# Inverting the delta-net chunk matrices: first level from a masked transpose, second factor turned by TensorE, level mask on the product

## The reference, cut to what matters

```
a = jnp.where(strict, einsum("bhnid,bhnjd->bhnij", kb, k) * decay, 0.0)
t_inv = triangular_solve(a + eye, eye, left_side=True, lower=True, unit_diagonal=True)
u = t_inv @ (v * beta[..., None])
w = t_inv @ (kb * jnp.exp(g)[..., None])
# then a scan over the chunks with the state s
```

## Time and profile before

| | us |
|---|---|
| median of three runs | 1910.13 (1909.71 to 1915.04) |
| the profiled execution, its own time | 1912.29 |
| its span | 1910.4 |
| PE, DVE, ACT, POOL busy in the span | 1774.9, 938.4, 631.0, 184.4 |
| first start and last end of the level products u, tt, ti | 1413.98, 1491.84 |
| first start of a `TT` product | 1492.48 |

### The profile page before, as it was taken

How to read it: one execution, slowest core, us unless ns; L and a number is a source line. 1 busy time by engine, 2 the same in 40 slices (tenths; PEclk the granted TensorE clock), 3 DMA queues, 4 the chain that set the end, 5 groups by cost and what they waited for, 6 DMA issues and landing times.

```text
span 1910.4 us, 25378 instructions
## 1 busy us (share of the span) xinstructions
PE 1774.9 (93%) x9992; PEld 1329.9 (70%) x9992; DVE 938.4 (49%) x1704; ACT 631.0 (33%) x1183; POOL 184.4 (10%) x202
## 2 busy tenths in 40 slices
PE   5999999899999999899989999899889789989998
PEld 2443445378888886343679998566579679879997
DVE  2134764343434343255636664444579853545544
ACT  3112643232313232134625443213322144034443
POOL 1001000100000001042000001001159100000000
PEclk8999999999999999999989999799899999999999
DMA  9224774322222232334034443223120234334442
GB/s 380 76 90 155 284 286 156 132 89 88 89 89 88 93 121 109 116 133 176 24 151 177 177 179 140 80 108 122 62 105 1 89 133 177 127 138 177 163 152 83
DMA packets 20885, 253.87 MB, mean 133 GB/s; under 512 B 2208, under 2 KB 4512, under 8 KB 5024
## 3 DMA queue, kind: packets, MB, share of 16 engines
q1 hardware_dynamic: 17712, 242.44, 33.4%
q10 hardware_dynamic: 3056, 9.82, 1.4%
HBM read 251.20 MB, written 1.05 MB: 132 GB/s over the span
## 4 chain that ended last, share of the span: by engine, by line
PE 84%; DVE 8%; ACT 3%; issue 2%; DMA 2%; POOL 1%; DVEq 0%; POOLq 0%; ACTq 0%
PE bank L491 26%; PE bank L517 13%; PE bank L519 13%; PE bank L518 13%; PE bank L912 6%; PE bank L575 3%; PE bank L649 3%; PE bank L672 2%; PE bank L657 2%; DVE w_lo L1558 1%; POOL root L2001 1%; ACT w_hi L1157 1%; DMA x<-in_x 1%; PE bank L628 1%; PE bank L636 1%
## 5 line engine op out<-in xcount | busy, mean ns | idle before, releaser
L491 PE MATMUL bank<-slab,weights 128*128 128x256 f32 (+2 forms) x1456 | 450.7, 469 | 8.2 <-ACT slab L1097 6.1
L491 PEld LDWEIGHTS bank<-slab,weights 128*128 128x128 f32 (+1 forms) x1456 | 277.5, 192 | 176.4 <-issue 142.8
L1558 DVE TENSOR_TENSOR w_lo<-weights,w_hi 128x1024 fp32r<-128x1024 f32 (+1 forms) x220 | 264.3, 1211 | 95.9 <-ACT w_hi L1157 95.0
L517 PE MATMUL bank<-h_hi,w_hi 128*128 128x256 f32 (+1 forms) x864 | 278.9, 323 | 25.4 <-DVE h_lo L1579 15.1
L1157 ACT ACTIVATE w_hi<-weights 128x1024 fp32r<-128x1024 f32 (+1 forms) x220 | 228.3, 1046 | 214.6 <-PE bank L519 209.5
L519 PE MATMUL bank<-h_hi,w_lo 128*128 128x256 f32 (+1 forms) x864 | 275.6, 319 | 0.0
L518 PE MATMUL bank<-h_lo,w_hi 128*128 128x256 f32 (+1 forms) x864 | 275.1, 318 | 0.0
L517 PEld LDWEIGHTS bank<-h_hi,w_hi 128*128 128x128 f32 x864 | 165.7, 192 | 41.1 <-issue 29.5
L517 PE MATMUL bank<-mlp_hidden_hi,w_hi 128*128 128x512 f32 (+1 forms) x512 | 174.8, 341 | 0.6 <-DVE w_lo L1558 0.6
L519 PEld LDWEIGHTS bank<-h_hi,w_lo 128*128 128x128 f32 x864 | 165.0, 191 | 12.8
L518 PEld LDWEIGHTS bank<-h_lo,w_hi 128*128 128x128 f32 x864 | 165.8, 192 | 11.6
(11 more groups left out here) (206 smaller groups left out, 2334.7 us busy)
## 6 DMA issues: line engine op xcount, KB each, us to landing
weights<-in_ada SPq DMA_DIRECT2D x36, 2048.0 KB, 7.6
weights<-in_mlp_up SPq DMA_DIRECT2D x16, 2048.0 KB, 8.5
weights<-in_mlp_down SPq DMA_DIRECT2D x16, 2048.0 KB, 8.4
weights<-in_ffn_in SPq DMA_DIRECT2D x11, 2048.0 KB, 7.6
weights<-in_in SPq DMA_DIRECT2D x8, 2048.0 KB, 8.3
weights<-in_gate SPq DMA_DIRECT2D x6, 2048.0 KB, 7.7
weights<-in_ffn_out SPq DMA_DIRECT2D x8, 1408.0 KB, 5.8
weights<-in_even_in SPq DMA_DIRECT2D x4, 2048.0 KB, 11.7
```

What stands on the lines that cost most here:

```text
L491: last = mm(b[rows, 0:width], lhsT(k), rhs(k), start=k == 0, stop=k == kc - 1)
L517: mm(b[:, 0:width], wh, hi(k), start=k == 0, stop=False)
L1558: V.tensor_tensor(split_part(w_lo, q), raw_part(q), split_part(w_hi, q).bitcast(F32), ALU.subtract)\
```

## The change

All in the inverse. (1) POOL's fill of X and Y with the identity is gone. (2) The first level is not run as a step: PE turns `Amat[:, t]` (group `a`), DVE writes `Y = -(turned) * between0` from the bank and adds the identity. (3) `X` is no longer kept: group `tr` turns Y by four transposes, and DVE writes `XR = tr * within` from the bank (`other_root`). (4) `lev` is gone: PE multiplies with the unmasked `Amat`, and the mask comes on the product, in the copy out of the bank, which DVE now does in ACT's place (`ubuf = u * between`). (5) POOL makes YR, in DVE's place. (6) `ti` and its subtraction are gone. 24 steps are left (`STEPS`).

```diff
+        STEPS = 4 * (len(LEVELS) - 1)
...
-            def level_products(n):
...
+            def turned(tag, src):
+                b = open_group(tag)
+                for hd in range(DN_HEADS):
+                    ins = nc.tensor.transpose(b[:, hs(hd)], src[:, hs(hd)], ident)
+                close(ins, tag)
+
+            def level_step(n):
+
+                if n < STEPS:
+                    t = n % 4
+                    pe.wait_ge(sem("YR_ready"), n + 1)
+                    heads(("u", n), lambda hd: Amat[:, t, hs(hd)], lambda hd: YR[:, n % 3, hs(hd)])
+                if 1 <= n <= STEPS:
+                    j = n - 1
+                    t = j % 4
+                    drained(pe, ("tr", j))
+                    drained(pe, ("u", j))
+                    heads(("tt", j), lambda hd: XR[:, t, hs(hd)], lambda hd: ubuf[:, j % 2, hs(hd)])
+                if 2 <= n < STEPS - 2:
+                    j = n - 2
+                    drained(pe, ("tt", j))
+                    turned(("tr", j + 4), Y[:, j % 4, :])
...
+            for t in range(4):
+                pe.wait_ge(sem("A_ready"), t + 1)
+                turned(("a", t), Amat[:, t, :])
+            for t in range(4):
+                pe.wait_ge(sem("Y_ready"), t + 1)
+                turned(("tr", t), Y[:, t, :])
+            for n in range(STEPS + 1):
+                level_step(n)
...
-                copy_out(("u", li, t), ubuf[:, n % 2, :])
...
+            filled(dve, ("vt", 3))
             for t in range(4):
+                filled(dve, ("a", t))
+                ins = V.scalar_tensor_tensor(out=by_head(Y[:, t, :]), in0=by_head(bank(("a", t))[:, :]), scalar=-1.0,
+                                             in1=level_mask("between", 0), op0=ALU.mult, op1=ALU.mult)
+                ins.then_inc(free(("a", t)), 1)
+                drained(dve, ("a", t))
+                V.tensor_tensor(by_head(Y[:, t, :]), by_head(Y[:, t, :]), spread(ident), ALU.add)\
+                    .then_inc(sem("Y_ready"), 1)
+
+            def other_root(n):
+
+                filled(dve, ("tr", n))
+                V.tensor_tensor(by_head(XR[:, n % 4, :]), by_head(bank(("tr", n))[:, :]), level_mask("within", n // 4 + 1),
+                                ALU.mult).then_inc(free(("tr", n)), 1)
+
+            filled(dve, ("f2", 3))
+            for n in range(4):
+                other_root(n)
+            for n in range(STEPS + 1):
+                if n < STEPS:
+                    filled(dve, ("u", n))
+                    if n >= 2:
+                        filled(dve, ("tt", n - 2))
+                    V.tensor_tensor(by_head(ubuf[:, n % 2, :]), by_head(bank(("u", n))[:, :]),
+                                    level_mask("between", n // 4 + 1), ALU.mult).then_inc(free(("u", n)), 1)
+                if n:
+                    filled(dve, ("tt", n - 1))
+                    V.tensor_tensor(Y[:, (n - 1) % 4, :], Y[:, (n - 1) % 4, :], bank(("tt", n - 1))[:, :], ALU.subtract)\
+                        .then_inc(free(("tt", n - 1)), 1)
+                if 2 <= n < STEPS - 2:
+                    other_root(n + 2)
...
+            for n in range(STEPS):
+                li, t = n // 4 + 1, n % 4
+                if li == 1:
+                    pool.wait_ge(sem("Y_ready"), t + 1)
+                else:
+                    drained(pool, ("tt", n - 4))
                 if n >= 3:
-                    filled(pool, ("u", *divmod(n - 3, 4)))
...
+                    filled(pool, ("u", n - 3))
+                nc.gpsimd.tensor_tensor(by_head(YR[:, n % 3, :]), by_head(Y[:, t, :]), spread("within", li), ALU.mult)\
+                    .then_inc(sem("YR_ready"), 1)
```

More of the change, by code:

```diff
@@ L320, in build @@
         diagG, zA, zB, zC = slots(0, 2), slots(2, 2), slots(4, 2), work[:, 6 * 512:7 * 512]
-        XR, YR, lev, ubuf = slots(0, 4), slots(4, 3), slots(7, 3), slots(10, 2)
+        XR, YR, ubuf = slots(0, 4), slots(4, 3), slots(10, 2)
         fu, fAS, sc_tmp = slots(7, 2), slots(9, 2), slots(11, 1).rearrange("p a b -> p (a b)").rearrange(
@@ L1369, in _ @@
                         act.wait_ge(sem("TT_ready"), 8)
-                        filled(act, ("tt", len(LEVELS) - 1, 3))
+                        filled(act, ("tt", STEPS - 1))
                     copy_out(("vn", d, s), VN[d])
@@ L1841, in _ @@
             link(V.memset(otok[:, :, :], 0.0))
[L1843 to L1868, removed]
-            for t in range(4):
-                drained(dve, ("tt", len(LEVELS) - 1, t))
+            def level_mask(name, li):
+                return spread(k2(name)[:, li * P:(li + 1) * P])
+            filled(dve, ("vt", 3))
+            for t in range(4):
+                filled(dve, ("a", t))
[5 more added lines that the diff above has]
+                    .then_inc(sem("Y_ready"), 1)
@@ L1871, in _ @@
+            for t in range(4):
+                drained(dve, ("tt", STEPS - 4 + t))
                 for d in range(2):
@@ L2018, in _ @@
             add_squares("mix2", TOK)
[L2019 to L2025, removed]
             def by_head(a):
@@ L2040, in _ @@
                                         ALU.mult).then_inc(sem("diag"), 1)
-            def level_part(n):
-                li, t = divmod(n, 4)
-                pool.wait_ge(sem("A_ready"), t + 1)
-                if n >= 3:
-                    filled(pool, ("u", *divmod(n - 3, 4)))
[L2048 to L2063, removed]
+            for n in range(STEPS):
[4 more added lines that the diff above has]
+                    drained(pool, ("tt", n - 4))
+                if n >= 3:
+                    filled(pool, ("u", n - 3))
+                nc.gpsimd.tensor_tensor(by_head(YR[:, n % 3, :]), by_head(Y[:, t, :]), spread("within", li), ALU.mult)\
+                    .then_inc(sem("YR_ready"), 1)
             add_squares("ffn", LAT)
```

## The result

The changed kernel takes 1889.03 us (median of four, 1887.11 to 1892.72) against 1909.92 (median of four, 1904.56 to 1915.04): ratio 0.9893, 95% interval 0.9862 to 0.9924. Timed a second time, five runs gave 1893.83 against 1909.35: 0.9917 (0.9903 to 0.9932). The forecast of 17.9 us less is a ratio of 0.9906, inside both intervals. The medians themselves differ by 20.9 us the first time and by 15.5 the second, so a whole time alone does not tell 17.9 from a few us more or less.

A forecast was written before the change was run, and what follows sets the result against it. POOL and DVE taking turns bound the inverse's step at 2.91 us. With PE as bound, 1419.9 + 52.2 + 1.7, then 0.2 and 0.6, gives 1474.6 against 1492.48: 17.9 us less, 1892.2 us, range 1886 to 1900.

The forecast's parts named there:

- What bounded the step: Inverse loop before: POOL 1.27, DVE about 0.5, POOL 1.27 us in turn make the 2.91 us step.
- bound of 0.121 us for a pass: Slow limit for PE's pace: the old step's 2.91 us over its 24 passes; it takes 3.9 us back.
- The step now: Changed loop: PE is the bound, 20 passes of 0.1125 us, 2.25 us a step in place of 2.91.
- Waits called covered: Changed loop: no new wait reaches PE; u's wait for YR covered by 2.8 us, tt's for masked u by 1.3.
- The entry: Ahead of the loop: chunks 1.92 us apart, u(0) at 1419.9 against 1413.98, a price of 5.9 us.
- The sign named for it: In the entry, additions of the identity take some 1.8 us for three of four.
- the collision: In the entry, DVE's identity additions wait 1.27 us for POOL's YR; without it 1.7 us less.
- The clock: At the entry PE's clock falls to half; 3.5 us at half clock lose 1.7 us, bounds 0 and 2.
- Rival 1: In the loop, transposes run one after the other at 0.273 us: step 2.89 us, 1905.0 us; chance 0.04.
- Rival 2: In the loop, POOL's product blocks DVE's bank readers too: step 3.07 us, 1911.9 us; chance 0.03.
- rival 3: In the loop the clock stays at half: step 4.50 us, 32.6 us later, 1942.7 us; chance 0.04.
- Nothing before or behind: Outside the inverse: what follows is the same work, not held up by weights; POOL's dropped identity copies give nothing back.

The follow-up runs named there:

- yr_on_dve: The changed kernel with YR made by DVE as before, POOL idle in the inverse: step 2.40 us, inverse stretch 66.2 us against 64.6.
- mask_on_factor: The changed kernel with POOL making lev from Amat again and ACT copying u out unmasked: step 2.47 us, inverse stretch 69.5 us against 64.6.
- old_no_lev: The kernel before without POOL's lev product, level mask left out, for timing only: step 2.68 us against 2.91, inverse stretch 77.4 us against 82.6.
- tr_product: The changed kernel with the loop's 20 transpose groups made as ordinary products with the identity: step 2.68 us, inverse stretch 73.7 us against 64.6.
- no_collision: The changed kernel with POOL's first YR waiting until all four Y are ready: step 2.22 us, inverse stretch 64.0 us against 64.6.
- busy_entry: The changed kernel with six idle identity products on PE ahead of each of the entry's four tr groups: inverse stretch 63.5 us against 64.6.
- short_entry: folded with two early masked copies, otok's clearing and kT's turning moved later, three XR between first u copies: inverse stretch 63.5 us, whole time 1886.87 us.
- short_entry_xr_first: short_entry with all four XR of the entry ahead of the first masked u copy again: inverse stretch 57.7 us, whole time 1887.30 us, ratio 0.9872.
- folded_again: The program of folded, profiled a second time, in the rounds of short_entry_xr_first: inverse stretch 60.2 us.
- folded: The changed kernel, identity subtracted from Amat as chunks are made, ones on first mask's diagonal: inverse stretch 60.2 us, whole time 1886.30 us, ratio 0.9876.

## Why the prediction was right

- **What bounded the step.** Right: POOL and DVE take turns. The three experiments on the pair show it from each side (yr_on_dve, mask_on_factor, old_no_lev). The sizes given for the turns, 1.27, 0.5 and 1.27, add up to 3.04 and not to the 2.91 of the step: POOL's products come 1.23 us apart, which leaves 0.45 for DVE. What the prediction did not say, though its rows held it, is how close PE stood behind: 2.68 us by old_no_lev. Its bound of 0.121 us for a pass, taken from the old step, was never PE's pace. (Its formula as written makes 0.108 of the 84 passes in 9.00 us; the 0.110 that it uses is 9.28/84.)
- **The step now.** Right: PE bound, 20 passes. A pass takes 0.111, not 0.1125, which is 0.7 us over 464 passes. tr_product shows the bound, yr_on_dve and mask_on_factor where the next ones lie: DVE 2.40 with a fourth operation, POOL 2.47 with a second.
- **Waits called covered.** Right: PE keeps its pace of 0.111 us in mid-loop, and DVE waits 0.20 us for each tt.
- **The entry.** Right: 1.92 us forecast from one addition to the next, 1.89 measured (1411.83 to 1413.72). The sign named for it, additions of some 1.8 us, was wrong: three of them take 1.25 to 1.26, since DVE's masked copy of 0.68 runs under the first half of POOL's product and only the rest is waited for. u(0) starts 10.4 us after the last Amat addition, forecast 10.1. But its terms are not independent, as no_collision shows: of 1.7 us for the collision only 0.6 can be had alone.
- **The clock.** Right that it falls: half from 1414.3 to 1421.1, 3.3 us of it under the loop's products (forecast 3.5). The first 40 passes took 6.19 us, some 1.6 more than at 0.111 each, near the 1.7 forecast. But keeping the clock full gives only 1.1 back (busy_entry), since DVE is late next. The entry had transposes and gaps together; which of the two let the clock fall no run tells apart.
- **The rivals.** Rival 1 (transposes one after the other) is out: four in 0.60 us with 0.27 of it the last one's length. The 275 ns that the page "TensorE: Matmul & The Clock Gate" of the Trainium skill (Part 4) gives from one kernel is about the length of a float32 record here (273), and the pace is 0.111. Rival 2 is out by mask_on_factor, rival 3 by the full clock of the loop from 1421.1 on.
- **Nothing before or behind.** Right within what can be seen: 82.6 - 64.6 = 18.0. The tails differ by 1.0 us, inside the 2.9 over which those of all fourteen profiles spread.
- **How near it came.** That 17.9 and 18.0 agree to 0.1 is partly luck: the entry came 0.4 us longer than forecast and the way from u(0) to the first TT product 0.5 shorter (54.2 in place of 54.7).

## What to carry to other kernels

Where VectorE and GpSimd work at the same time and operations of one kind are longer there than elsewhere (here 1.79 us in place of 0.68), look which VectorE operations have both inputs in SBUF. Giving one of them an input in a bank ended the wait here (0.69 us under POOL's products). Then see what stands right behind (here PE, 0.23 us a step away). Count a 128x128 float32 product as two passes and a transpose as one (0.11 us each here), and trade products for transposes where a factor is another's transpose. In an entry with short waits the terms are not additive: an earlier start can be partly paid at half clock (0.6 of 1.2 us in no_collision), and an operation moved forward in one queue must not leave a bank undrained that another queue asks for sooner (5.8 us between short_entry and short_entry_xr_first).

## What was not expected of the hardware

- POOL's float32 products over 128x512 follow each other at 1.23 us while each spans 1.28 (mask_on_factor).
- The half clock after a thin stretch lasted 3.3, 4.5 and 3.5 us into steady products (after; no_collision; before at 1498.47), so its price depends on when the products begin.
- In folded_again the mean clock from the gate sums to the inverse was 0.93 in place of 0.88, and that stretch 3.7 us shorter, with the program of folded. The two traces put most of it down to one fall of the clock, near 1333 in folded, that folded_again alone of the fourteen profiles has not; why is open.
